# A chunked delta rule: the inverse turned by VectorE's 32x32 transposition, and the query norm folded into the guard of the output's norm

## What is computed

```python
q = l2_norm(q) * 128 ** -0.5          # x * rsqrt(sum(x*x) + 1e-6)
k = l2_norm(k)
m = strict_lower(k_beta @ k.T * decay)
t_inv = solve(eye + m, eye)           # unit lower triangular
attn_intra = lower(q @ k.T * decay)
# per chunk:
v_new = t_inv @ v_beta - (t_inv @ (k_beta * exp(g))) @ state
o = (q * exp(g)) @ state + attn_intra @ v_new
state = state * g_last + k_dec.T @ v_new
# behind it:
o = rms_norm(o, out_norm) * silu(z)   # x * rsqrt(mean(x*x) + 1e-6) * gain
```

## Time and profile before

| | |
|---|---|
| median of 3 runs | 1512.96 us (1512.95 to 1517.23) |
| profiled execution | 1513.9 us, span of its instructions 1512.1 us |
| TensorE busy | 1470.8 us, 97% |
| VectorE, ScalarE, GpSimd busy | 578.0, 599.5 and 558.1 us |
| granted TensorE clock | 0.998 of full speed |
| delta rule, eight heads | about 118.7 to 466 us of the span |

### The profile page before, as it was taken

How to read it: one execution, slowest core, us unless ns; L and a number is a source line. 1 busy time by engine, 2 the same in 40 slices (tenths; PEclk the granted TensorE clock), 3 DMA queues, 4 the chain that set the end, 5 groups by cost and what they waited for, 6 DMA issues and landing times.

```text
span 1512.1 us, 23620 instructions
## 1 busy us (share of the span) xinstructions
PE 1470.8 (97%) x9048; PEld 1185.3 (78%) x9048; DVE 578.0 (38%) x1066; ACT 599.5 (40%) x1020; POOL 558.1 (37%) x270
## 2 busy tenths in 40 slices
PE   6989999999999999999999999999999999999998
PEld 5867777777786788888888887776788888888887
DVE  2555666566674422221022224576422221022210
ACT  5634545434553433322223234586434232232322
POOL 4532221332312344444533444222254444434442
PEclk9999999999999999999999999999999999999999
DMA  6322101111101133223322224111133323323232
GB/s 234 133 72 71 43 31 55 57 45 54 46 20 32 53 118 111 84 94 89 124 85 96 83 79 138 49 54 43 43 110 103 111 75 96 122 84 101 77 96 75
DMA packets 39227, 124.23 MB, mean 82 GB/s; under 512 B 4192, under 2 KB 5472, under 8 KB 39136
## 3 DMA queue, kind: packets, MB, share of 16 engines
q1 hardware_dynamic: 38976, 122.68, 25.2%
q10 hardware_dynamic: 160, 0.26, 0.1%
HBM read 120.57 MB, written 2.10 MB: 81 GB/s over the span
## 4 chain that ended last, share of the span: by engine, by line
PE 92%; DVE 3%; ACT 2%; issue 1%; DMA 0%; DVEq 0%; SPq 0%; ACTq 0%
PE bank L591 75%; PE bank L775 2%; PE bank L793 2%; ACT ws L1169 1%; PE bank L796 1%; PE bank L965 1%; DVE ws L1639 1%; PE bank L924 1%; DVE act_lo L1636 1%; PE bank L758 1%; PE bank L1101 1%; PE bank L603 1%; PE bank L954 1%; PE bank L830 1%; PE bank L1125 1%
## 5 line engine op out<-in xcount | busy, mean ns | idle before, releaser
L538 POOL TENSOR_TENSOR w_lo<-w_raw,w_hi 128x1024 fp32r<-128x1024 f32 (+1 forms) x250 | 537.9, 2168 | 790.9 <-ACT w_hi L1169 790.9
L591 PE MATMUL bank<-act_hi,w_hi 128*128 128x512 f32 (+1 forms) x1776 | 708.3, 399 | 6.7 <-DVE act_lo L1636 2.6
L591 PE MATMUL bank<-act_hi,w_lo 128*128 128x512 f32 (+1 forms) x1776 | 680.6, 383 | 0.0
L591 PE MATMUL bank<-act_lo,w_hi 128*128 128x512 f32 (+1 forms) x1776 | 679.5, 383 | 0.0
L591 PEld LDWEIGHTS bank<-act_hi,w_hi 128*128 128x128 f32 x1776 | 335.4, 189 | 77.2 <-issue 8.6
L591 PEld LDWEIGHTS bank<-act_hi,w_lo 128*128 128x128 f32 x1776 | 335.0, 189 | 66.0
L591 PEld LDWEIGHTS bank<-act_lo,w_hi 128*128 128x128 f32 x1776 | 335.9, 189 | 60.5 <-issue 4.1
L1169 ACT ACTIVATE w_hi<-w_raw 128x1024 fp32r<-128x1024 f32 (+1 forms) x250 | 230.7, 953 | 89.0 <-PE bank L591 86.9
L1630 DVE TENSOR_TENSOR ws<-bank,ws 128x512 f32<-128x512 f32 x110 | 75.8, 690 | 334.9 <-PE bank L591 324.8
L1169 ACT ACTIVATE ws<-ws 128x512 f32<-128x512 f32 (+2 forms) x121 | 78.5, 651 | 148.8 <-DVE ws L1630 111.8
L1957 DVE TENSOR_TENSOR xT<-xT,bank 128x512 f32<-128x512 f32 (+1 forms) x48 | 33.0, 687 | 257.0 <-PE bank L591 257.0
(11 more groups left out here) (170 smaller groups left out, 1124.7 us busy)
## 6 DMA issues: line engine op xcount, KB each, us to landing
w_raw<-w_stream SPq DMA_DIRECT2D x154, 512.0 KB, 3.2
w_raw<-w_out SPq DMA_DIRECT2D x32, 384.0 KB, 3.1
w_raw<-w_down SPq DMA_DIRECT2D x32, 384.0 KB, 3.1
w_raw<-w_down SPq DMA_DIRECT2D x32, 320.0 KB, 3.2
ws<-x_in SPq DMA_DIRECT2D x1, 2048.0 KB, 8.3
ws<-mem_in SPq DMA_DIRECT2D x2, 512.0 KB, 4.7
out<-ws SPq DMA_DIRECT2D x1, 1024.0 KB, 4.2
out<-ws SPq DMA_DIRECT2D x1, 768.0 KB, 3.7
```

The source lines that it names most:

```text
L538: nc.gpsimd.tensor_tensor(w_lo[:, s, 0:width * P], w_raw[:, s, 0:width * P], w_hi[:, s, 0:width * P].bitcast(F32), ALU.subtract).then_inc( ...
L591: mm = nc.tensor.matmul(acc, wt[:, c % RING, wsl], at[:, act0(k0 + k), off:off + n], start=(start and k == 0 and m == 0), stop=(stop and k ...
```

## The change

1. In levels 1 to 4 VectorE turns T by its transposition of 32x32 blocks (`V.transpose`, semaphore `y_done`) and no longer TensorE by L796; ahead of level 1 it does so in place of L753 and ScalarE's copy. While the blocks are at most 32x32, this gives the whole transpose. Each subtraction of levels 1 to 4 covers T alone, 128 columns. T's step of the next level waits for `y_done`.
2. Queries aren't normed. L758 and GpSimd take CQ as it is. The query's square, scaled by 128·sqrt(eps), goes into tile QN (`square_q`), and VectorE adds it to the squares of the output (`o_sum`), ahead of the sums over features; the constant `eps_o` = 128·eps² is the rest of the guard. Query sums, their rounding and split, and the root of them go.
3. The output's sums (`output_sums`) of head h-1 stand behind L745 of head h, the split and `o_finish` later in VectorE's order, the root (`o_root`) in ScalarE's. The last head sums in f32 at its end, as before.
4. GpSimd makes EG before the lower part of the last head's output. CQ is overwritten once L758, GpSimd and the query's square have read it.

```diff
@@ -82 +82 @@
-                      ("sinks", SW_HEADS), ("nslope", SW_HEADS), ("eps", 1), ("ln_q", 1), ("ln_s", 1),
+                      ("sinks", SW_HEADS), ("nslope", SW_HEADS), ("eps", 1), ("ln_q", 1), ("ln_s", 1), ("eps_o", 1),
...
@@ -430,0 +431,6 @@
+        Y_PER_HEAD = 1 + 2 * (LEVELS - 3)
+
+        def y_count(k, g):
+
+            return 1 if k == 0 else 2 * (k - 1) + g + 2
+
@@ -555,0 +562,3 @@
+                pool.wait_ge(S.eg_done, h + 1)
+                pool.wait_ge(S.c_ready, 2 * h + 1)
+                nc.gpsimd.tensor_tensor(w(EG), w(EG), w(CQ), ALU.mult).then_inc(S.qd_done, 1)
@@ -558,4 +566,0 @@
-
-                pool.wait_ge(S.eg_done, h + 1)
-                pool.wait_ge(S.qn_done, h + 1)
-                nc.gpsimd.tensor_tensor(w(EG), w(EG), w(QN), ALU.mult).then_inc(S.qd_done, 1)
...
@@ -708,5 +713,2 @@
-                pe.wait_ge(S.sq_done, 2 * h + 2)
-                if h == 0:
-                    nc.tensor.matmul(psum(D[0]), sq(ONES), w(E0), start=True, stop=True).then_inc(S.ss_done, 1)
-                    return
-                two_part_sums(D[0], act_hi[:, SUM_T, :], act_lo[:, SUM_T, :]).then_inc(S.ss_done, 1)
+                pe.wait_ge(S.osq_lo, h + 1)
+                two_part_sums(D[0], act_lo[:, OHI_T, :], act_lo[:, OLO_T, :]).then_inc(S.oss, 1)
...
@@ -732 +732,0 @@
-                    pe.wait_ge(S.o_ln, h)
@@ -746,0 +747,2 @@
+                if due(h):
+                    output_sums(h - 1)
@@ -749,8 +751,3 @@
-                pe.wait_ge(S.z_done, h + 1)
-                pe.wait_ge(S.dm_pre, h + 1)
-                for t in range(NT):
-                    for r in range(2):
-                        mm = nc.tensor.matmul(bank[half_rows(r), D[2], HB * t:HB * (t + 1)], packed(TT, t, r, 1),
-                                              sq_c[half_rows(r), IDENT, HB * r:HB * (r + 1)], start=True, stop=True)
-                mm.then_inc(S.t_tr, 1)
-                pe.wait_ge(S.qn_done, h + 1)
+                pe.wait_ge(S.c_ready, 2 * h + 1)
+                if due(h):
+                    pe.wait_ge(S.o_ln, h)
@@ -758 +755 @@
-                    mm = nc.tensor.matmul(bank[:, D[0], t * P:(t + 1) * P], tt(KN, t), tt(QN, t), start=True, stop=True)
+                    mm = nc.tensor.matmul(bank[:, D[0], t * P:(t + 1) * P], tt(KN, t), tt(CQ, t), start=True, stop=True)
@@ -766 +763,2 @@
-                            pe.wait_ge(S.t_done, 2 * h + 2)
+                            pe.wait_ge(S.t_done, h + 1)
+                            pe.wait_ge(S.y_done, Y_PER_HEAD * h + 1)
@@ -780,0 +779,2 @@
+                        if k < LEVELS - 1:
+                            pe.wait_ge(S.y_done, Y_PER_HEAD * h + y_count(k - 1, g))
@@ -793,2 +793,4 @@
-                                nc.tensor.matmul(bank[half_rows(r), D[4 + g], HB * i:HB * (i + 1)],
-                                                 packed(TT, t, r, 1), packed(PM, t, r), start=True, stop=True)
+                                mm = nc.tensor.matmul(bank[half_rows(r), D[4 + g], HB * i:HB * (i + 1)],
+                                                      packed(TT, t, r, 1), packed(PM, t, r), start=True, stop=True)
+                            if k < LEVELS - 2:
+                                continue
@@ -837 +838,0 @@
-                    query_sums_dn(h + 1)
@@ -839,4 +839,0 @@
-
-                if h + 1 == DN_HEADS:
-                    pe.wait_ge(S.osq, 2 * h + 1)
-                    nc.tensor.matmul(psum(D[2]), sq(ONES), w(E1), start=True, stop=True).then_inc(S.oss, 1)
@@ -844,2 +841,3 @@
-                pe.wait_ge(S.osq_lo, h + 1)
-                two_part_sums(D[2], act_lo[:, OHI_T, :], act_lo[:, OLO_T, :]).then_inc(S.oss, 1)
+
+                pe.wait_ge(S.o_sum, h + 1)
+                nc.tensor.matmul(psum(D[2]), sq(ONES), w(E1), start=True, stop=True).then_inc(S.oss, 1)
@@ -1277 +1275,3 @@
-                        act.wait_ge(S.qn_done, h)
+                        act.wait_ge(S.gg_done, 2 * h)
+                        act.wait_ge(S.qd_done, h)
+                        act.wait_ge(S.q_sq, h)
...
@@ -1318,10 +1318,4 @@
-                if isinstance(h, int) and h == 0:
-                    a(w(E0), w(CQ), ACT.Square).then_inc(S.sq_done, 1)
-                    return
-                act.wait_ge(S.at_done, h)
-                a(psum(D[0]), w(CQ), ACT.Square).then_inc(S.sq_hi, 1)
-
-            def round_q(h):
-                act.wait_ge(S.sq_hi, 4 * h - 1)
-                act.wait_ge(S.ss_done, 2 * h + 1)
-                a(act_hi[:, SUM_T, :], psum(D[0]), ACT.Copy).then_inc(S.sq_hi, 1)
+                act.wait_ge(S.c_ready, 2 * h + 1)
+                if due(h):
+                    act.wait_ge(S.o_sum, h)
+                a(w(QN), w(CQ), ACT.Square, scale=P * math.sqrt(EPS)).then_inc(S.q_sq, 1)
...
@@ -1334,0 +1329,9 @@
+            def o_root(h, sums):
+
+                act.wait_ge(S.oss, h + 1)
+                if due(h):
+                    act.wait_ge(S.o_t2, h)
+                a(w(E1), psum(sums), ACT.Ln, scale=1.0 / P, bias=col("eps_o")).then_inc(S.o_ln, 1)
+                act.wait_ge(S.o_ln, h + 1)
+                a(w(E1), w(E1), ACT.Exp, scale=-0.5).then_inc(S.o_rstd, 1)
+
@@ -1344,2 +1347 @@
-                act.wait_ge(S.ss_done, 2 * h + 2)
-                a(w(E0), psum(D[0]), ACT.Ln, bias=col("eps")).then_inc(S.rr_ln, 1)
+                square_q(h)
@@ -1351,2 +1353,2 @@
-                act.wait_ge(S.rr_ln, 2 * h + 2)
-                a(psum(D[0]), w(E0), ACT.Exp, scale=-0.5, bias=col("ln_q")).then_inc(S.rr_done, 1)
+                if due(h):
+                    o_root(h - 1, D[0])
@@ -1356,2 +1357,0 @@
-                act.wait_ge(S.t_tr, h + 1)
-                a(w(TT)[:, 0:SEQ // 2], psum(D[2], SEQ // 2), ACT.Copy).then_inc(S.t_done, 1)
...
@@ -1379,5 +1376 @@
-                if following:
-                    a(psum(D[2]), psum(D[5]), ACT.Square).then_inc(S.osq, 1)
-                    act.wait_ge(S.osq, 2 * h + 1)
-                    a(act_lo[:, OHI_T, :], psum(D[2]), ACT.Copy).then_inc(S.osq, 1)
-                else:
+                if not following:
@@ -1385,6 +1378,8 @@
-                if following:
-                    rr_k(h + 1)
-                act.wait_ge(S.oss, h + 1)
-                a(w(E1), psum(D[2]), ACT.Ln, scale=1.0 / P, bias=col("eps")).then_inc(S.o_ln, 1)
-                act.wait_ge(S.o_ln, h + 1)
-                a(w(E1), w(E1), ACT.Exp, scale=-0.5).then_inc(S.o_rstd, 1)
+                    o_root(h, D[2])
+                    return
+                a(psum(D[0]), psum(D[5]), ACT.Square).then_inc(S.osq, 1)
+                rr_k(h + 1)
+                act.wait_ge(S.o_sum, h + 1)
+                if due(h):
+                    act.wait_ge(S.oss, h)
+                a(act_lo[:, OHI_T, :], psum(D[0]), ACT.Copy).then_inc(S.osq, 1)
...
@@ -1777,4 +1770,0 @@
-            def split_q(h):
-                dve.wait_ge(S.sq_hi, 4 * h)
-                sub(act_lo[:, SUM_T, :], psum(D[0]), hi(SUM_T)).then_inc(S.sq_done, 1)
-
...
@@ -1800 +1790 @@
-                    o_finish(h - 1)
+                    split_o(h - 1)
@@ -1816,2 +1806,4 @@
-                dve.wait_ge(S.rr_done, 2 * h + 2)
-                mul(w(QN), w(CQ), psum(D[0])).then_inc(S.qn_done, 1)
+                dve.wait_ge(S.z_done, h + 1)
+                V.transpose(w(TT)[:, 0:SEQ // 2], w(TT)[:, SEQ // 2:]).then_inc(S.y_done, 1)
+                if due(h):
+                    o_finish(h - 1)
@@ -1837,3 +1829 @@
-                            both = w(TT).rearrange("p (f g c) -> p f g c", f=2, g=2)[:, :, g, :]
-                            sub(both, both, psum(D[4 + g], 2 * P).rearrange("p (f c) -> p f c", f=2)
-                                ).then_inc(S.tz_done, 1)
+                            sub(w(TT)[:, own], w(TT)[:, own], psum(D[4 + g], P)).then_inc(S.tz_done, 1)
@@ -1850,0 +1841,7 @@
+                    if k < LEVELS - 2:
+                        for g in range(2):
+                            dve.wait_ge(S.tz_done, PER_HEAD * h + tz_count(k, g))
+                            own = slice(P * g, P * (g + 1))
+                            V.transpose(w(TT)[:, SEQ // 2 + P * g:SEQ // 2 + P * (g + 1)], w(TT)[:, own]
+                                        ).then_inc(S.y_done, 1)
+
@@ -1874,4 +1871 @@
-                if following:
-                    split_q(h + 1)
-                    split_o(h)
-                fill(3)
+                squares_ = psum(D[0]) if following else w(E1)
@@ -1878,0 +1873,3 @@
+                dve.wait_ge(S.q_sq, h + 1)
+                V.tensor_tensor(squares_, squares_, w(QN), ALU.add).then_inc(S.o_sum, 1)
+                fill(3)
...
@@ -2146 +2145 @@
-         everywhere(np.array([EPS, -0.5 * math.log(P), -0.5 * math.log(SW_DIM)], np.float32)),
+         everywhere(np.array([EPS, -0.5 * math.log(P), -0.5 * math.log(SW_DIM), P * EPS * EPS], np.float32)),
```

More of the change, by code:

```diff
@@ L230, in yoco_kernel @@
             z_done = sem("z_done")
[L231 removed]
             t_done = sem("t_done")
```

(35 more changed lines are left out.)

17 lines of the change are left out of this document (5 added, 12 removed).

## The result

| | before | after |
|---|---|---|
| median | 1512.95 us (4 runs, 1512.78 to 1517.23) | 1494.25 us (4 runs, 1491.65 to 1495.17) |
| ratio | | 0.9867, 95% interval 0.9846 to 0.9888 |
| profiled execution | 1513.9, span 1512.1 | 1494.14, span 1492.3 |
| TensorE busy, instructions | 1470.8, 9048 | 1450.0, 8392 |
| granted clock, mean | 0.998 | 0.991 |

A forecast was written before the change was run, and what follows sets the result against it. TensorE, busy 97% of the span, was taken as the bound. Gains of 3.35 (head 0), 6 x 2.95 and 0.96 (last head) make 22.0, less 0.7: 21.3 us off 1512.96 gives 1491.7, range 1489 to 1501.

The forecast's parts named there:

- TensorE's part of a middle head, 2.95: Middle head of 44.74 us: TensorE sheds 0.61 for level 0's turning, 1.88 in levels 1 to 4, 0.46 for query sums.
- nothing gained: Output sums (0.26 and 0.23) only move from behind the value transposes to behind L745, so TensorE saves nothing on them.
- The transpositions, 0.29 and 0.21 apart: VectorE in levels 1 to 4: each 128-column transposition lasts 0.29 us, the next operation starting 0.21 after its start.
- The third tap: VectorE's convolution tap behind level 2 ends at 3.54 us; TensorE's projection 2 wants its psum bank at 3.62.
- the 0.1 a head booked for it: Loss allowed for the tight tap before projection 2, 0.04 spare after semaphore time; 0.7 us over seven heads.
- priced 1.7 us: If VectorE's next operation waited for an empty pipe, the tap would end 0.25 later, costing seven heads 1.7 us; left out.
- The output sums, "spare 0.1": Behind L745 at the head border: split ends 2.06 us after L735, L745 ends at 2.18, so no loss.
- case A of the rivals: Transpositions near their upper bound or the output sums' split late: 2 to 10 us lost, 1494 to 1502; chance 0.20.
- Head 0, 3.35: First head gains 0.61 and 1.88 from the turning and 0.86 from its f32 query sums, 3.35 us.
- Last head, 0.96: Last head nets 0.96 us: 0.46, 0.61 and 0.96 gained, 0.35 lost on a copy, 0.72 on the sum of squares.
- Rival B (GpSimd holds the transpositions): Transpositions wait for GpSimd's w_lo: slower, 1519 in full (chance 0.04), 1507 with one collision (0.05).
- Rival C: L793 alone still takes the old 1.08 us a level, so only 8 to 9 us gained, 1504; chance 0.03.

The follow-up runs named there:

- x0: The changed kernel run once more without any edit, as yardstick for the runs beside it: median 1491.77 us, 0.9860 of before.
- x1: The changed kernel with the turning given back to TensorE and only the folded query norm kept: 1513.46 us, 0.9999 of before.
- x8: The kernel before with only the turning by VectorE, no query folded and no output sum moved: 1497.95 us, 0.9887 of before.
- x2: The changed kernel with each VectorE transposition of levels 1 to 4 done twice: 1495.62 us, 0.9882 of before.
- x3: The changed kernel with each VectorE transposition of levels 1 to 4 done three times: 1504.29 us, 0.9939 of before.
- x6: The changed kernel with VectorE splitting the output's squares before the decay sum and not after it: 1490.02 us, 0.9830 of before.

## Why the prediction was right

Its mechanism holds, and so do its numbers step by step, but for one spare that was misread and for the last head. The total was met within 2.6 us in the first set of runs and within 0.1 in the second, and the 0.1 is partly luck: the steps measured at full clock give 3.54 + 6 x 2.96 + 1.7 = 23.0 us and not 21.3, and the clock falls of some runs take a part of that back (1513.32 - 1491.77 = 21.6 by the medians of x0's set).

- **TensorE's part of a middle head, 2.95:** measured 2.96. x1 and x8 divide it. Each term was right (0.61 for L753, 0.47 for a level, 0.46 for the query sums), and two that were not in the sum cancelled: the query product came down from 1.09 to 0.89, and the output sums grew by 0.18. In x1, where the 16 turning products of 64 columns stand ahead of it again, it takes 1.09 again. The output sums were put at "nothing gained"; behind L745 they cost more than at their old place, by the wait of the third point.
- **The transpositions, 0.29 and 0.21 apart:** 0.287 and 0.20. The nearest row was the right price. The third tap ended 0.13 before the eighth's issue where 0.08 was forecast (0.04 of it for the semaphore), and 0.06 before the load of its first weights, which the forecast didn't look at; the 0.1 a head booked for it was not lost. x2 and x3 show that the place decides as it was described. The Trainium skill (VectorE: DVE Perf Modes, The DRAIN you can't avoid), by which the prediction priced 1.7 us, says that the next operation waits for the emptied pipe, and adds that one that isn't held starts earlier. These rows show the second: two transpositions of 0.29 take 0.50 together.
- **The output sums, "spare 0.1":** wrong by 0.3. The split ended when forecast (205.20 + 0.68 = 205.88, 2.05 behind L735's end at 203.83), and L745's issue too (206.00, 2.17). The failed step is that the spare was read up to that end: the sums' left operand (the ones) is loaded as weights behind the same wait, and in x6, where nothing keeps it back, that load starts 0.27 before L745's issue ends (206.62 against 206.89). Here it was wanted at 205.73 and started at 205.93, 0.05 behind the split. The order of x6 won 0.24 a head. This is case A of the rivals, in a small size, and it was hidden from the total by the cheaper query product: that the 2.95 came out as 2.96 is luck in this part.
- **Head 0, 3.35:** from the start of the key sums (118.72 before, 117.53 after) to the issue end of the last output product (163.04 and 158.31) 44.32 to 40.78, so 3.54. The 0.19 more is the query product again.
- **Last head, 0.96:** 1.7 at full clock (x0, from the last output product of head 6 to the last output sums: 33.44 to 31.77). The sum of squares cost 0.72 as forecast, the copy ahead of the first masking 0.27 (0.35). The levels were 1.68 and not 1.81, as the masking follows the first subtraction by 0.86 and not by 1.0: 1.54 in four levels where 0.96 was forecast. In the first profile 3.3 us of half clock turned the gain into a loss of 1.6; no step of the prediction had a clock in it.
- **Rival B (GpSimd holds the transpositions)** is out by the 64 rows, of which 18 pairs run beside GpSimd's w_lo. The Trainium skill (GPSIMD Engine Reference, 1. Specifications) names only VectorE instructions with two SBUF inputs or in a 2-port mode as colliding with GpSimd, and the rows agree: the transposition has one input and isn't held.
- **Rival C** is out: L793 alone took 0.61.

What is open: why the granted clock falls in the last head in some executions and not in others.

## What to carry to other kernels

Where TensorE is busy throughout, a transposition that VectorE can do in 32x32 blocks is worth the whole issue time that TensorE spent on it, as long as it fits between two waits; read that room at each place of the cycle, and not from the engine's idle share (13.9 us idle in a middle head of the changed kernel, less than 0.1 us of room). A step that is folded away is worth little by itself if its engine wasn't late, and more once something else is put in its place (here 1.1 and 2.7 us). A spare ahead of a product has to be read up to the load of its weights, which the wait keeps back as well. Compare two versions by intervals of their profiles when the total holds clock falls that come and go.

## What the hardware did that was not expected

- One and the same kernel ran its last head at a granted clock of 1.00 in one execution and at 0.50 for stretches in another (0.50 at 434 to 438 us, 0.53 at 442 to 446), with 3.3 us between them. In front of it TensorE had been busy for 74, 84 and 67% of three stretches of 3 to 4 us in both.
- A VectorE transposition of 128x128 f32 took 287 ns at the median, as an elementwise operation with psum does, and 256 columns 446; from SBUF to SBUF it was not held by GpSimd's two-input subtraction, unlike the two-input operation of the earlier trace rows.
